# Output units between the steps of a mixing loop, and overlapped convolutions in a delta layer

## The reference

```python
def hybrid_mixer(hn, w_in, ...):
    z, xbc, dt_raw, sc_b, sc_c, sc_v = jnp.split(hn @ w_in, ...)
    xbc = jax.nn.silu(causal_depthwise_conv(xbc, ssd_conv_w) + ssd_conv_b)
    xs, bm, cm = jnp.split(xbc, ...)
    y = ssd_chunked_scan(xh, dt, a, bm, cm) + d_skip * xh
    ssd_out = grouped_rmsnorm(y * jax.nn.silu(z), ssd_norm, SSD_GROUPS)
    sc = sc_b * causal_depthwise_conv(sc_c * sc_v, sc_conv_w)
    sc_out = grouped_rmsnorm(sc, sc_norm, SC_GROUPS)
    return jnp.concatenate([ssd_out, sc_out], axis=-1) @ w_out

def gdn_mixer(xn, w_in, conv_w, ...):
    qkv, z, a, b = jnp.split(xn @ w_in, ...)
    qkv = jax.nn.silu(causal_conv(qkv, conv_w))
    q, k, v = jnp.split(qkv, ...)
    q = jnp.repeat(l2_norm(q), rep, axis=2) * d ** -0.5
    k = jnp.repeat(l2_norm(k), rep, axis=2)
    ...   # decays, triangular inverse, two-chunk recurrence, norm, gate
```

## Time and profile before

| | |
|---|---|
| median of 3 runs | 1422.6 us |
| profiled execution: time, span | 1421.43 us, 1419.6 us |
| busy: TensorE, VectorE, ScalarE | 1147.6, 653.0, 421.7 us |
| mixing layer and output projection | 0 to 250 us |
| experts | 250 to about 740 us |
| delta layer's projections | about 1045 to 1133 us |
| read from HBM | 310.42 MB |
| one block of weights | 2 DMAs of 1024 KB |

### The profile page before, as it was taken

How to read it: one execution, slowest core, us unless ns; L and a number is a source line. 1 busy time by engine, 2 the same in 40 slices (tenths; PEclk the granted TensorE clock), 3 DMA queues, 4 the chain that set the end, 5 groups by cost and what they waited for, 6 DMA issues and landing times. The chain is left out here.

```text
span 1419.6 us, 20644 instructions
## 1 busy us (share of the span) xinstructions
PE 1147.6 (81%) x8606; PEld 881.9 (62%) x8606; DVE 653.0 (46%) x1233; ACT 421.7 (30%) x641; POOL 6.1 (0%) x28
## 2 busy tenths in 40 slices
PE   4999879776565665566569999998899869799998
PEld 4999768422121221212139989888789868789887
DVE  4786676410101101010136458665557856454576
ACT  3544333100000000000025436453145433155353
POOL 1000000000000000000000000000000000000000
PEclk9999999898888989989899999999699989899999
DMA  8465214999999999999986532453043410046400
GB/s 275 125 239 202 96 45 162 395 408 409 410 410 409 410 409 410 410 410 410 410 342 192 178 108 94 156 178 119 0 163 135 138 42 3 1 127 179 146 26 30
DMA packets 119657, 312.62 MB, mean 220 GB/s; under 512 B 17059, under 2 KB 17290, under 8 KB 119578
## 3 DMA queue, kind: packets, MB, share of 16 engines
q1 hardware_dynamic: 116864, 310.78, 58.9%
q10 hardware_dynamic: 2714, 0.71, 0.2%
HBM read 310.42 MB, written 1.05 MB: 219 GB/s over the span
## 5 line engine op out<-in xcount | busy, mean ns | idle before, releaser
L1092 DVE TENSOR_TENSOR w_l<-ring,w_h 128x1024 fp32r<-128x1024 f32 x204 | 246.5, 1223 | 150.0 <-ACT w_h L634 148.3
L634 ACT ACTIVATE w_h<-ring 128x1024 fp32r<-128x1024 f32 x204 | 213.6, 1057 | 235.9 <-PE bank L2057 134.4
L2284 PE MATMUL bank<-ring,cm 128*32 128x512 f32 x960 | 148.8, 751 | 115.4 <-DMA ring<-in_w_up 69.2
L2284 PEld LDWEIGHTS bank<-ring,cm 128*32 128x32 f32 x960 | 29.1, 126 | 228.2 <-DMA ring<-in_w_up 94.9
L2050 PE MATMUL bank<-hnT_h,w_h 128*128 128x256 f32 x992 | 143.1, 287 | 6.4 <-DVE cm L1056 3.1
L2054 PE MATMUL bank<-hnT_l,w_h 128*128 128x256 f32 x992 | 140.7, 285 | 0.0
L2057 PE MATMUL bank<-hnT_h,w_l 128*128 128x256 f32 x992 | 140.0, 284 | 0.0
L2050 PEld LDWEIGHTS bank<-hnT_h,w_h 128*128 128x128 f32 x992 | 129.2, 193 | 10.2 <-DVE cm L1056 3.4
L2054 PEld LDWEIGHTS bank<-hnT_l,w_h 128*128 128x128 f32 x992 | 129.3, 194 | 0.0
L2057 PEld LDWEIGHTS bank<-hnT_h,w_l 128*128 128x128 f32 x992 | 128.8, 193 | 0.0
L2305 PE MATMUL bank<-ring,cm 128*32 128x512 f32 x496 | 68.9, 694 | 47.6 <-DMA ring<-in_w_down 42.8
(11 more groups left out here) (414 smaller groups left out, 1399.1 us busy)
## 6 DMA issues: line engine op xcount, KB each, us to landing
ring<-in_w_down SPq DMA_DIRECT2D x62, 1024.0 KB, 15.8
ring<-in_w_gate SPq DMA_DIRECT2D x60, 1024.0 KB, 14.6
ring<-in_w_up SPq DMA_DIRECT2D x60, 1024.0 KB, 15.7
ring<-in_fox_w_in SPq DMA_DIRECT2D x32, 1024.0 KB, 9.7
ring<-in_w_in SPq DMA_DIRECT2D x22, 1024.0 KB, 8.6
ring<-in_gla_w_in SPq DMA_DIRECT2D x12, 1024.0 KB, 6.2
ring<-in_gdn_w_in SPq DMA_DIRECT2D x12, 1024.0 KB, 6.3
ring<-in_w_out SPq DMA_DIRECT2D x8, 1024.0 KB, 6.3
```

Of the source, the lines that this page charges most:

```text
L634: af(part(w_h, u, width), w, ACT.Copy).then_inc(s["high_ready"], 1)
L1092: v.tensor_tensor(part(w_l, u, width), w, part(w_h, u, width).bitcast(F32), ALU.subtract).then_inc(s["low_ready"], 1)
L2284: x = mm(bank[a][CAP * e:CAP * (e + 1), :], m_xg[:, 2 * b + r, CAP * e:CAP * (e + 1)], expert_of(w, e)[:, r * FF:(r + 1) * FF], start=(b = ...
```

## The change

In the mixing layer the sums of squares of sc move between blocks 9 and 10, the spreads between the units of block 10, the roots and `sc_pair` beside them. The low and high halves of sc's outputs are made pair by pair before and in the loop. Of sc's 8 output units one is placed before the loop and seven behind its steps 0, 1, 1, 2, 3, 4 and 6, in banks 4 to 7. One residual addition stands in step 2, the first gating in step 6. The gated half's sums move behind its first four units.

In the delta layer the linear parts of the convolutions use two buffers in turn (`g_lin`). Silu of group k - 1 follows the bank copies of group k. Both halves of the sums of squares stand behind block 3, the roots behind the fourth group's taps, and the spreads behind each unit of block 5, with the rescalings beside them. The last two bank copies come last. The halves are asked for in another rhythm.

```diff
+SC_OUT_BANKS = ((4, 5), (6, 7))
+SSD_OUT_BANKS = (((0, 1), (2, 3)), ((6, 7), (1, 5)))
+SC_UNITS_BEHIND = {0: (1,), 1: (2, 3), 2: (4,), 3: (5,), 4: (6,), 6: (7,)}
+SC_UNITS_AFTER_EXP = {1: 4, 2: 5, 3: 6, 4: 7, 5: 8}
+        g_lin = [vtm[:, 0, :], hnTf[:, 0:1024]]
...
 # ScalarE, mixing layer
             for b in range(16):
                 copy_bank("ssd", 6 + b, ...)
                 ssd_tanh(6 + b)
+                if b in (12, 13):
+                    act.wait_ge(s["ssd_conv_done"], b - 8)
+                    squares("sc", b - 12, ...)
+            act.wait_ge(s["spread_used"], 4)
+            for p in range(4):
+                out_high("ssd", p, tiles(36 + 2 * p, 2))
...
                 if i == 1:
                     silu_z(0, 2)
+                if i in SC_UNITS_AFTER_EXP:
+                    high(first + SC_UNITS_AFTER_EXP[i])
             for k in range(2):
                 act.wait_ge(s["ssd_yready"], k + 1)
+                for p in (2 * k, 2 * k + 1):
+                    act.wait_ge(s["unit_done"], first + UNITS + p + 1)
...
+                    i.then_inc(s["out_high"], 1)
+                    high(first + 2 * UNITS + p + 1)
                 act.wait_ge(s["z_ready"], 2)
                 squares("ssd", k, ...)
+            high(first + 4 * UNITS)
...
 # ScalarE, delta layer
+                for k in range(4):
+                    n = bank_units("gdn", 2 * k + 1)
+                    high(n + 2)
                     act.wait_ge(s["proj_copied"], PROJ_BASE["gdn"] + 2 * k + 2)
-                    if k:
-                        act.wait_ge(s["gdn_conv_done"], k)
                     for i in range(4):
+                        x = af(g_lin[k % 2][:, i * T:(i + 1) * T], cm[:, 4 * k + i, :], ACT.Copy, scale=vec[:, w:w + 1])
                     x.then_inc(s["gdn_tap"], 1)
+                    high(n + 3)
                     if 1 <= k <= 2:
                         act.wait_ge(s["gdn_conv_done"], k)
                         squares("gdn_qk", k - 1, tf(4 * (k - 1), 4))
+                    high(n + 5)
+                    act.wait_ge(s["lin_ready"], 3 + k + 1)
+                    if k:
+                        act.wait_ge(s["gdn_conv_done"], k)
+                    af(vtm[:, 1, :], g_lin[k % 2], ACT.Tanh).then_inc(s["tanh_ready"], 1)
...
 # VectorE, mixing layer
+            low(UNIT_BASE["ssd"] + UNITS * 10 + 1)
+            row_roots("sc", 16, 1.0 / 64)
+            for b in range(4):
+                low(UNIT_BASE["ssd"] + UNITS * 10 + b + 2)
+                sc_pair(b)
             low(UNIT_BASE["ssd_out"] + PARTS)
             for k in range(4):
+                if k == 2:
+                    out_low("ssd", 0, tiles(36, 2))
                 ...
             segment(0)
+            out_low("ssd", 1, tiles(38, 2))
...
                 decayed(i)
                 if i == 0:
-                    row_roots("sc", 16, 1.0 / 64)
-                if i == 1:
+                    out_low("ssd", 2, tiles(40, 2))
                     ...
+                    out_low("ssd", 3, tiles(42, 2))
+                if i in SC_UNITS_AFTER_EXP:
+                    low(first + SC_UNITS_AFTER_EXP[i])
                 if i == 2:
+                    sc_added(0)
+                if i == 3:
                     silu_z("ssd", 0)
-                if i >= 4:
-                    sc_pair(i - 4)
-            out_low("ssd", 0, tiles(36, 8), 4)
-            gated(0)
+                if i == 6:
+                    gated(0)
+            for p in (0, 1):
+                y_low(p)
+                low(first + 2 * UNITS + p + 1)
             dve.wait_ge(s["ssd_yready"], 1)
             gated(1)
+            sc_added(1)
             dve.wait_ge(s["ssd_yready"], 2)
+            for p in (2, 3):
+                y_low(p)
+                low(first + 2 * UNITS + p + 1)
+            low(first + 3 * UNITS + 1)
             row_roots("ssd", 2, 1.0 / BLK)
...
 # VectorE, delta layer
+                def gdn_banks(k):
+                    for b in (2 * k, 2 * k + 1):
+                        scaled_copy("gdn", b, tf(2 * b, 2), None if k < 4 else 0.5, 2)
+                def gdn_taps(k):
+                    n = bank_units("gdn", 2 * k + 1)
+                    low(n + 3)
+                    dve.wait_ge(s["proj_copied"], PROJ_BASE["gdn"] + 2 * k + 2)
+                    dve.wait_ge(s["gdn_tap"], k + 1)
+                    for d in (1, 2, 3):
+                        ...
+                        if d < 3:
+                            link(x)
+                            low(n + 3 + d)
+                    x.then_inc(s["lin_ready"], 1)
+                    low(n + 6)
+                def gdn_silu(k):
+                    dve.wait_ge(s["lin_ready"], 3 + k + 1)
+                    dve.wait_ge(s["tanh_ready"], 3 + k + 1)
+                    v.scalar_tensor_tensor(out=tf(4 * k, 4), in0=vtm[:, 1, :], scalar=1.0, in1=g_lin[k % 2], ...)
+                gdn_banks(0)
+                gdn_taps(0)
...
                 for k in (1, 2, 3):
-                    gdn_conv(k)
+                    gdn_banks(k)
+                    gdn_silu(k - 1)
+                    gdn_taps(k)
+                    if k == 3:
+                        row_roots("gdn_qk", 8, 1.0)
+                gdn_banks(4)
+                gdn_silu(3)
...
+                for b in range(4):
+                    low(UNIT_BASE["gdn"] + 5 * UNITS + b + PARTS)
+                    dve.wait_ge(s["spread_done"], SPREAD_BASE["gdn_qk"] + b + 1)
+                    ...
+                dve.sem_inc(s["gdn_qk_ready"], 1)
+                low(UNIT_BASE["gdn_out"] + PARTS)
+                for b in (10, 11):
+                    scaled_copy("gdn", b, tf(2 * b, 2), 0.5)
...
 # TensorE, mixing layer
-            project("ssd", 3, 11)
+            project("ssd", 3, 10)
+            sum_squares("sc", 16, lambda i: colsel64[:, i, :])
+            project("ssd", 10, 11, lambda m: m and spread("sc", 16, ..., [m - 1] if m < 3 else [2, 3]))
...
             ssd_spread(0)
             ssd_spread(1)
-            sum_squares("sc", 16, lambda i: colsel64[:, i, :])
+            sc_unit(0)
+            ...
             for i in range(8):
                 pe.wait_ge(s["ssd_m"], i + 1)
+                if i in (2, 3):
+                    pe.wait_ge(s["ssd_added"], i - 1)
                 ...
                 if i < 6:
                     ssd_spread(i + 2)
+                for k in SC_UNITS_BEHIND.get(i, ()):
+                    sc_unit(k)
-            out_projection("ssd", [0])
...
 # TensorE, delta layer
                 project("gdn", 3, 4)
+                pe.wait_ge(s["rbc_ready"], LATE.index("gdn") + 1)
+                sum_squares("gdn_qk", 8, lambda i: column(i, 8))
                 project("gdn", 4, 5)
-                sum_squares("gdn_qk", 8, lambda i: column(i, 8), [0])
-                project("gdn", 5, 6)
-                sum_squares("gdn_qk", 8, lambda i: column(i, 8), [1])
-                spread("gdn_qk", 8, lambda i: [i])
+                project("gdn", 5, 6, lambda m: spread("gdn_qk", 8, lambda i: [i], [m]))
```

More of the change, by code:

```diff
@@ L1046, in rstd_spread, with scaled_copy @@
                 dve.wait_ge(s["rbc_ready"], LATE.index(name) + 1)
-            def scaled_copy(layer, b, dst, scale=None):
+            def scaled_copy(layer, b, dst, scale=None, ahead=PARTS):
                 g = PROJ_BASE[layer] + b
                 done = bank_units(layer, b)
-                low(min(done + PARTS, UNIT_BASE[layer + "_out"] + PARTS))
+                low(min(done + ahead, UNIT_BASE[layer + "_out"] + PARTS))
                 dve.wait_ge(s["unit_done"], done)
@@ L1375, in gated, with sc_added, y_low @@
                 v.tensor_tensor(tf(8 + 4 * k, 4), tf(8 + 4 * k, 4), tf(4 * k, 4), ALU.mult).then_inc(s["ssd_yready"], 1)
+            first = UNIT_BASE["ssd_out"]
+            def sc_added(n):
+                dve.wait_ge(s["unit_done"], first + UNITS * (n + 1))
+                for t in range(NT):
+                    c = slice(n * BLK, (n + 1) * BLK)
+                    v.tensor_tensor(x_res[:, t, c], bank[SC_OUT_BANKS[n][t]][:], x_res[:, t, c], ALU.add).then_inc(s["ssd_added"], 1)
+            def y_low(p):
+                dve.wait_ge(s["out_high"], PAIR_BASE["ssd"] + 4 + p + 1)
+                for j in (0, 1):
+                    c = VCOL["ssd_norm"] + 2 * p + j
+                    x = v.scalar_tensor_tensor(out=hnT_l[:, 2 * p + j, :], in0=cm[:, 8 + 2 * p + j, :], scalar=vec[:, c:c + 1],
+                                               in1=hnT_h[:, 2 * p + j, :].bitcast(F32), op0=ALU.mult, op1=ALU.subtract)
+                x.then_inc(s["out_low"], 1)
             segment(0)
+            out_low("ssd", 1, tiles(38, 2))
             dve.wait_ge(s["ssd_dte_step"], 2)
@@ L2082, in gate_unit, with project @@
                 channel_unit(bank[2 + h % 2][:, 0:T], UNIT_BASE[name] + UNITS * FOX_Z + h)
-            def project(name, first, end):
+            def project(name, first, end, after=None):
                 for i in range(first, end):
```

(25 more changed lines are left out.)

95 lines of the change are left out of this document (32 added, 63 removed).

## The result

The changed kernel took 1426.5 us, median of 20 runs (1422.8 to 1433.6); the kernel before, beside it on the same chip, 1421.0 us (20 runs, 1411.9 to 1426.8). The ratio is 1.0048, 95% interval 1.0035 to 1.0062: **slower by 5 to 9 us**. I had said 13, with a range that began at 1424.

What follows compares the result with a forecast made beforehand. The expert stage was held bound by full DMA from a trigger paced by TensorE, the delta steps by VectorE. Mixing +5 and delta +8 gave 13 us over the profiled 1421.4, or 1435 as median; range 1424 to 1441.

Steps and rivals of the forecast that it cites:

- Mixing layer, +5: Mixing layer: the load that triggers the expert weight stream comes at 249.6 instead of 244.70, costing 5 us.
- Two terms behind the loop: Mixing layer after its loop: gated half's sums at 234.6 to 238.2, then a serial chain to the last split, trigger 249.6.
- the charge for the lower clock: Mixing layer, units after the gated half's sums: a lower TensorE clock adds 1.2 us before the last split.
- every clock charge: Mixing layer: three lower-clock charges, 1.7 us after the first sums, 1 after idle time, 1.2 after the gated half's sums.
- The reading of the Trainium skill: Mixing layer, first unit of block 10: if any issuing counts as activity, no clock drop, 1.7 us less.
- Delta layer, +8: Delta layer: decays come 7.1 to 9.2 us later, at 1156.8 to 1158.9 against 1149.7; taken as 8 us.
- The tail from there to the decays: Delta layer, from the fourth linear part at 1134.9: roots, three units, four spreads and last copies until decays at 1156.8 to 1158.9.
- the upper end of the tail: Delta layer: three units and four spreads take up to 15 us instead of 12.9, with the lower clock after idle time.
- What follows only moves along: After the delta layer's decays: the rest of that layer and the last layer only shift, adding no time.
- Rival (c): Delta layer comes out even, its steps bound by VectorE either way and last three units hidden: 1428 us, chance 0.10.
- (a): Delta layer gains about 9 us, roots being ready for the first spread: 1418 us in all, chance 0.08.
- Rival (b): Mixing loop gains: TensorE's 12.4 us of idle time filled, trigger 4 us earlier: 1427 us, chance 0.12.

Runs made afterwards that it cites:

- the delta part alone: The kernel before with only the delta layer's part of the change, mixing layer as before: 1427.5 us against 1419.2, ratio 1.0060.
- the high halves came early: Only the delta layer's part of the change on the kernel before, with two ScalarE high halves per step made earlier: 1416.5 us against 1419.2, ratio 0.9976.
- the later low halves: Whole change with both high halves early, plus two mixing-layer low halves put behind the scaling of values, run twice: 1410.5 and 1409.3 us, ratios 0.9920 and 0.9906.

## Why the prediction was off

The direction holds, and so does the mechanism in the delta layer. The mixing layer's +5 is the step that failed: its single events came close to the forecast, but the part costs nothing. The total came out about twice too large. By its steps:

- **Mixing layer, +5: mis-sized, measured -0.3** (103.0 to 102.7, stage means). Counted from the stage's start, the steps came out close: first values 28.4, forecast 27.3; TensorE's idle time before them 3.86, forecast 4; loop end 77.6, forecast 77.0. The low clock began earlier than charged: the first unit behind the sums is slow as forecast (2.05 for its first pass), but the second half of the sums is slow too, and they end at 6.2, forecast 4.6. Two terms behind the loop were too large: the gated half's sums end at 92.9, forecast 93.9, and the last split 9.4 later, forecast 11.4, of which 1.2 was the charge for the lower clock. That one comes in two traces of four and makes 1 us of the stage (103.2 and 103.3 against 102.2 and 102.3). Together, 3.0 less, this takes the +5 to the +1.9 to +2.9 of the traces against the one of before. What is left is the base of the sum: the trace that I reckoned from is 2.6 us below the mean of eight. I had put every clock charge on the new order and left the old one at what a single trace shows, while it has a long form of its own, 105.6 us at 0.89, in half of them.
- The reading of the Trainium skill ("TensorE: Matmul & The Clock Gate", What's actually happening) by which any issuing is activity foretold no drop behind such sums. The drop at 147.8 says little on it, since 0.94 us of idle time stand in those sums. The earlier trace rows speaks against it, where the sums ran without a pause, but the same place in the new order, at 237.9, took 1.19 in one execution and 2.05 in another of the same program. Neither reading is a rule to charge by in full: of the 1.2 us charged there, two of the four traces show about 1 and two show none.
- **Delta layer, +8: right in kind, +4.7 in size** (112.0 against a mean of 107.3). Two waits for a high half in each step, forecast 1.6 and 2.2, are 1.66 and 2.07. But a step is 15.76, not 16.3, since VectorE's work in it is 12.0 us and not 12.4 (a split's row says 1.23, and the next instruction starts 1.14 behind its start). So the fourth linear part came 0.2 us earlier in the stage than before instead of 1.6 later: this is the term of the +8 that is gone. The tail from there to the decays I had at 21.9 to 24.0, and it is 21.4 against 16.4 before. The first spread starts 5.5 us behind the fourth linear part, exactly as forecast; that TensorE idles 2.79 us before it and not 5.6 only says that TensorE arrived later. No slow units came behind it (the pass in front of it takes 1.12, the last spread 1.05), so the upper end of the tail was not needed.

```profile
1128.09 1.12 PE L2116 MATMUL bank<-hnT_h,w_l 128*128 128x256 f32 x8
...
1143.38 1.05 PE L2191 MATMUL bank<-ident,heads 128*128 128x128 f32 x8
```

- **What follows only moves along: not quite.** Behind the decays the change has 272.8 and 275.9 us, the kernel before 269.8, 274.2 and 274.1: +1.7 in the mean. This is within what single traces differ by there. The prediction had no such term; over all traces it looks real, and in size it is open.
- Sum of the stage means: -0.3 + 4.7 + 1.7 is 6, beside the 5 to 9 measured in the first comparison; the change run again gave -1 to +5. This leaves out the stretch between the stages, where the change has 788.4 and 791.3 us and the kernel before 797.8, 790.2 and 791.1, 3 less in the mean, by one long trace. That the sum of 6 fits is in part luck. So is how near the +8 comes to the median of the delta part alone (+8.3): only 4.7 of it arise in the stage that was charged.

Rival (c), a delta layer that comes out even, and (a), one that gains, were both false for this code. The price of (a) was nearly met once the high halves came early (7.4 us in the stage against 9): the overlap of the buffers does what it promises when the queue of splits is not held behind tanh. Rival (b) gives almost the measured time, 1427, but by luck: it had the trigger 4 us earlier, and in the new order it came at 102.2 to 103.3 us into the stage where the old one has 100.3 to 105.7.

## What to carry to other kernels

When an in-order engine both prepares inputs for another's queue and waits for that queue's result, put the preparation ahead of the wait: here one line that moves a 1.06 us copy ahead of tanh is worth 8.6 us of a 112 us stage, since it takes a wait of 2.07 us from each of four steps of the engine that sets the pace. Before costing a change of half a per cent, take several traces of the kernel before and compare stage by stage; a single one can be a stage's short form. Check as well which execution was traced, since it can lie 8 us from the median. And compare what lies behind the stage too: here it was up to 4 us longer at a lower granted clock, for reasons that these runs do not show.

## What was unexpected of the hardware

The same instruction stream has two lengths in the mixing stage, 100.5 and 105.6 us, with granted clocks 0.95 and 0.89, and they occur in equal number in eight traces. Behind the delta layer the length moves with the clock as well, from 269.8 (0.96) over 274.2 (0.94) to 278.0 (0.93), with VectorE busy 151.5 to 151.6 us in each. It was longest in the kernels whose delta stage was shortest: five such traces have 277.4 to 278.0 and one has 272.6, so this is frequent and not fixed.

Narrow sums and the level of 1.2 GHz go together, but not always. In the first sums of the new order the clock fell behind half of the products (1.85 us) and 0.94 us of idle time, in all six traces that have them. At the gated half's sums, 32 products of 2 columns without a pause, it fell during or right behind them in seven of the eight traces of the old order, in two of the four of the new one and in both with the later low halves. The same pass of the same program took 1.19 us in one execution and 2.05 in another. In the delta layer of the change the sums are 32 products of 8 columns in a row, and the passes right behind them took 1.49, 1.91 and 1.61 us instead of 1.12, at a granted clock of 0.59 from 1113.2 to 1117.4. Slow passes follow these sums in all ten traces with a new delta order:

```profile
1109.59 3.64 PE L2172 MATMUL bank<-onehot,sq 128*128 128x8 f32 x32
1113.09 1.49 PE L2109 MATMUL bank<-hnT_h,w_h 128*128 128x256 f32 x8
1114.38 1.91 PE L2113 MATMUL bank<-hnT_l,w_h 128*128 128x256 f32 x8
1116.08 1.61 PE L2116 MATMUL bank<-hnT_h,w_l 128*128 128x256 f32 x8
```
